# Routed experts with the weights as stationary operand: gate and up over 256 moving rows, gate factor applied when the result is copied

## What is computed

```python
def step(acc, blk):
    tok, g, e = blk                                  # 128 rows of one expert, their gates
    xb = xpad[tok]                                   # gather, 128 x 1024
    hid = jax.nn.silu(xb @ w_gate[e]) * (xb @ w_up[e])   # 128 x 256
    yb = (hid @ w_down[e]) * g[:, None]              # 128 x 1024
    return acc.at[tok].add(yb.astype(acc.dtype)), None
```

## Time and profile before

| | |
|---|---|
| median of 3 runs | 2429.33 us (2426.62 to 2432.03) |
| the profiled execution | 2434.02 us, span 2432.3 us |
| PE busy | 2247.8 us, 92% of the span |
| mean granted TensorE clock | 0.958 of 2.4 GHz |
| routed experts, steady part | about 1170 us to 2330 us |
| in it: PE, DVE, ACT, POOL busy | 100%, 64%, 59%, 37% |

### The profile page before, as it was taken

The page is one execution under the profiler, slowest core; times in us unless marked ns, Lnnn a source line. Parts: engine busy times, 40 slices in busy tenths (PEclk is TensorE's granted clock), DMA queues, the critical chain, the costliest instruction groups (busy, mean ns, idle before and its releaser), DMA issues. The chain is left out here.

```text
span 2432.3 us, 34810 instructions
## 1 busy us (share of the span) xinstructions
PE 2247.8 (92%) x10992; PEld 1825.9 (75%) x10992; DVE 1418.9 (58%) x2627; ACT 1115.7 (46%) x1803; POOL 649.8 (27%) x550
## 2 busy tenths in 40 slices
PE   7999999999949999984999999999999999999940
PEld 5777777777737888873888888888888888888840
DVE  5343334434346877773666666666666666666638
ACT  4342323334233333321555565565556655655533
POOL 1000000000011322332333343333333433333326
PEclk9999999999979999996999999999999999999975
DMA  5001000001372322324899999998999999899946
GB/s 207 32 32 37 26 33 26 33 26 34 110 182 80 104 95 79 102 78 157 261 281 287 284 276 283 286 277 278 282 291 271 284 281 290 270 287 283 286 115 241
DMA packets 198657, 435.85 MB, mean 179 GB/s; under 512 B 39584, under 2 KB 44176, under 8 KB 197296
## 3 DMA queue, kind: packets, MB, share of 16 engines
q1 hardware_dynamic: 155024, 289.49, 35.7%
q0 software_dynamic: 43600, 145.95, 22.4%
HBM read 328.16 MB, written 109.39 MB: 180 GB/s over the span
## 5 line engine op out<-in xcount | busy, mean ns | idle before, releaser
L1573 PE MATMUL ex_psU<-ex_guh,ex_xh 128*128 128x512 f32 x1024 | 411.4, 402 | 4.2 <-DVE ex_xl L1558 4.2
L1575 PE MATMUL ex_psU<-ex_guh,ex_xl 128*128 128x512 f32 x1024 | 402.1, 393 | 0.0
L1574 PE MATMUL ex_psU<-ex_gul,ex_xh 128*128 128x512 f32 x1024 | 401.4, 392 | 0.0
L1546 DVE TENSOR_TENSOR ex_gul<-ex_raw,ex_guh 128x1024 fp32r<-128x1024 f32 x256 | 299.2, 1220 | 41.1 <-ACT ex_guh L1496 41.1
L1422 POOL DMA_INDIRECT acc_d<-ex_y,ex_use x128 | 207.3, 1619 | 399.4 <-ACT ex_y L1485 343.6
L1496 ACT ACTIVATE ex_guh<-ex_raw 128x1024 fp32r<-128x1024 f32 x256 | 253.5, 1060 | 31.6 <-DMA ex_raw<-w_experts 31.6
L1573 PEld LDWEIGHTS ex_psU<-ex_guh,ex_xh 128*128 128x128 f32 x1024 | 193.5, 189 | 41.3 <-DVE ex_xl L1558 4.8
L1575 PEld LDWEIGHTS ex_psU<-ex_guh,ex_xl 128*128 128x128 f32 x1024 | 193.3, 189 | 41.0
L1574 PEld LDWEIGHTS ex_psU<-ex_gul,ex_xh 128*128 128x128 f32 x1024 | 193.8, 189 | 37.1
L1444 POOL DMA_INDIRECT ex_xg<-h_d,ex_ent x128 | 198.0, 1547 | 68.1 <-issue 38.1
L1573 PE MATMUL ex_psY<-ex_dnh,ex_hdh 128*128 128x512 f32 x512 | 210.3, 411 | 1.7 <-DVE ex_hdl L1529 1.7
(11 more groups left out here) (298 smaller groups left out, 4354.5 us busy)
## 6 DMA issues: line engine op xcount, KB each, us to landing
ex_raw<-w_experts SPq DMA_DIRECT2D x192, 1024.0 KB, 11.7
acc_d<-de_acc SPq DMA_DIRECT2D x19, 512.0 KB, 3.0
mi_xr<-xT SPq DMA_DIRECT2D x17, 512.0 KB, 3.5
de_cr<-cat SPq DMA_DIRECT2D x17, 512.0 KB
de_xr<-x_rows SPq DMA_DIRECT2D x17, 512.0 KB, 4.4
h_d<-de_h POOLq DMA_DIRECT2D x17, 512.0 KB, 6.2
ln_t<-acc_d SPq DMA_DIRECT2D x8, 1024.0 KB, 6.7
y<-ln_z SPq DMA_DIRECT2D x8, 1024.0 KB, 4.9
```

What stands on the lines that cost most here:

```text
L1546: V.tensor_tensor(lo, src, hi.bitcast(F32), ALU.subtract).then_inc(s_split, 1)
L1573: nc.tensor.matmul(out, lh, rh, start=start, stop=False)
L1574: nc.tensor.matmul(out, lh, rl, start=False, stop=False)
L1575: return nc.tensor.matmul(out, ll, rh, start=False, stop=stop)
```

## The change

The loop is written anew per expert instead of per block.

- Gate and up: the weights (`ex_guh`, `ex_gul`, 128x128) are now the stationary operand, and the 256 rows of both blocks (`ex_xh`, `ex_xl`) move. 96 matmuls of 256 columns per expert stand for 48 of 512. The result `ex_psU` has hidden units on partitions, in two halves `f`.
- Hidden is thereby already laid out as `down` wants it: the transposes L1581 and the tile `ex_psH` are gone. ACT rounds hidden out of SBUF.
- The gate no longer enters in VectorE's multiply. It is the scale of ACT's copy of `ex_psY` to `ex_y`, which is now four pieces of 512 columns per expert.
- `ex_xh`/`ex_xl` exist once for both blocks, no longer one per block parity; `ex_psX` exists twice, `ex_psY` has two halves that are handed over singly.
- PE's order per expert e: gate and up of e-1 (second half), the transposes of both blocks of e, down of e-2 (both blocks), gate and up of e (first half).
- The queues of POOL and SP keep their order.

```diff
-        psX, psU = ps("psX", [P, D]), ps("psU", [P, 2, 2 * FF])
-        psH, psY = ps("psH", [P, FC * P]), ps("psY", [P, D])
+        psX, psU, psY = ps("psX", [P, 2, D]), ps("psU", [P, FC, 2, BLK]), ps("psY", [P, 2, D // 2])
...
             def add_expert(e, b):
 
                 hold(pool, s_use, e + 1, s_passed)
                 for t in range(2):
-                    add_rows(2 * e + t, 2 * b + t)
+                    hold(pool, s_y, 4 * e + 2 * t + 2, s_passed)
+                    nc.gpsimd.indirect_dma_start(
+                        out=io["acc_d"], out_offset=bass.IndirectOffsetOnAxis(ap=use[:, 2 * b + t, 0:1].bitcast(U32), axis=0),
+                        in_=y[:, 2 * b + t, :], in_offset=None, compute_op=ALU.add).then_inc(s_add, 16)
...
+            def output(e, b, units):
+                if exists(e):
+                    for u in units:
+                        k, half = 2 * b + u // 2, u % 2
+                        act.wait_ge(s_dn, 4 * e + u + 1)
+                        if u == 0:
+                            act.wait_ge(s_use, e + 1)
+                            after(act, s_add, 32 * (e - 1))
+                        A(y[:, k, half * 512:(half + 1) * 512], psY[:, half, :], ACT.Copy,
+                          scale=use[:, k, 1:2].bitcast(F32)).then_inc(s_y, 1)
+
+            def pair(p, j):
+                for b in range(2):
+                    e = 2 * p + b
+                    sigmoid(e - 1, 0)
+                    round_w(p, e, b, (0, 1))
+                    hidden(e - 1, 0, 1 - b)
+                    round_w(p, e, b, (2, 3))
+                    sigmoid(e - 1, 1)
+                    round_x(e, 0)
+                    hidden(e - 1, 1, 1 - b)
+                    round_x(e, 1)
+                    output(e - 2, b, range(4))
+                    round_w(p, e, b, (4, 5))
...
-            def hidden_T(m, k):
-                pe.wait_ge(s_hid, m + 1)
-                pe.wait_ge(s_hl, m)
-                for f in range(FC):
-                    last = nc.tensor.transpose(psH[:, f * P:(f + 1) * P], hid[:, k % 2, f * P:(f + 1) * P], ident[:])
-                last.then_inc(s_hT, 1)
...
+            def transpose_x(p, e, b):
+                for t in range(2):
+                    pe.wait_ge(s_row[2 * b + t], 16 * (p + 1))
+                    after(pe, s_xl, 2 * e + t - 1)
+                    for kc in range(KC):
+                        last = nc.tensor.transpose(psX[:, t, kc * P:(kc + 1) * P], xg[:, 2 * b + t, kc * P:(kc + 1) * P], ident[:])
+                    last.then_inc(s_xT, 1)
...
-                    last = three(psU[:, k % 2, :], xh[:, k % 2, kc, :], xl[:, k % 2, kc, :],
-                                 guh[:, b, kc, :], gul[:, b, kc, :], kc == 0, kc == KC - 1)
+                for half in range(2):
+                    c0 = half * FF + f * P
+                    for kc in range(KC):
+                        last = three(psU[:, f, half], guh[:, b, kc, c0:c0 + P], gul[:, b, kc, c0:c0 + P],
+                                     xh[:, kc].rearrange("p s t -> p (s t)"), xl[:, kc].rearrange("p s t -> p (s t)"),
+                                     kc == 0, kc == KC - 1)
...
+            def pair(p, j):
+                for b in range(2):
+                    e = 2 * p + b
+                    gate_up(e - 1, 1 - b, 1)
+                    transpose_x(p, e, b)
+                    down(e - 2, b)
+                    gate_up(e, b, 0)
```

More of the change, by code:

```diff
@@ L1354, in stage_experts, with piece @@
         s_gu, s_sig, s_hid = sem("gate_up"), sem("sig"), sem("hid")
[L1355 to L1363, removed]
+        s_hh, s_hl, s_dn = sem("hid_hi"), sem("hid_lo"), sem("down")
+        def piece(b, q):
+            kind, part = q // 2, q % 2
             src = raw[:, b, kind, part * 1024:(part + 1) * 1024]
@@ L1369, in piece, with pairs @@
             return src, dnh[:, b, part, :], dnl[:, b, part, :]
[L1371 to L1376, removed]
+        def pairs(eng, pair):
+            for p in range(2):
+                pair(p, None)
+            with eng.Fori(2, PAIRS) as p:
+                pair(p, None)
             more = eng.value_load(ov[0:1, 2 * OVMAX:2 * OVMAX + 1], min_val=0, max_val=OVP)
@@ L1441, in pair @@
                         k = 2 * b + t
-                        if not first:
+                        if not (early and p == 0):
                             hold(pool, s_xT, 4 * p + k - 3, s_passed)
@@ L1523, in _ @@
+            e = 2 * pairs(act, pair)
+            sigmoid(e - 1, 0)
+            hidden(e - 1, 0, 1)
+            sigmoid(e - 1, 1)
+            output(e - 2, 0, range(2))
+            hidden(e - 1, 1, 1)
+            output(e - 2, 0, range(2, 4))
+            output(e - 1, 1, range(4))
         @block.vector
@@ L1568, in _ @@
+            e = 2 * pairs(dve, pair)
+            for f in range(FC):
+                activate(e - 1, f)
+                hidden(e - 1, f, 1)
         @block.tensor
@@ L1601, in down @@
+            def down(e, b):
+                if not exists(e):
+                    return
+                pe.wait_ge(s_hl, 2 * e + 2)
+                pe.wait_ge(s_split, 6 * e + 6)
+                for u in range(4):
+                    t, half = u // 2, u % 2
+                    after(pe, s_y, 4 * e + u - 1)
                     for f in range(FC):
-                        last = three(psY[:, cols], hdh[:, f, :], hdl[:, f, :], dnh[:, b, f, cols], dnl[:, b, f, cols],
+                        last = three(psY[:, half, :], hdh[:, b, f, t * P:(t + 1) * P], hdl[:, b, f, t * P:(t + 1) * P],
+                                     dnh[:, b, f, half * 512:(half + 1) * 512], dnl[:, b, f, half * 512:(half + 1) * 512],
@@ L1627, in _, with pair @@
-            end = pairs(pe, pair)
-            n = 4 * end
-            hidden_T(n - 2, 2)
-            gate_up(n - 1, 3, 1, 12 * end - 2)
-            down(n - 2, 1, 12 * end)
-            hidden_T(n - 1, 3)
-            down(n - 1, 1, 12 * end)
+                    last.then_inc(s_dn, 1)
+            def pair(p, j):
+                for b in range(2):
+                    e = 2 * p + b
+                    gate_up(e - 1, 1 - b, 1)
+                    transpose_x(p, e, b)
+                    down(e - 2, b)
+                    gate_up(e, b, 0)
@@ L1637, in stage_norm @@
+            e = 2 * pairs(pe, pair)
+            gate_up(e - 1, 1, 1)
+            down(e - 2, 0)
+            down(e - 1, 1)
 def stage_norm(nc, io):
```

209 lines of the change are left out of this document (75 added, 134 removed).

## The result

The changed kernel takes 2460.43 us (median; 2459.43 to 2463.49), the kernel before 2430.14 us beside it: ratio 1.0128, 95% interval [1.0111, 1.0146]. It is slower by 30 us, where 110 were forecast.

The account below looks back on a forecast made before the run. PE bounds the kernel before; a once-per-expert ring through adds and gathers was to replace it. (20.45 - 18.62) x 61 = 112 us, ends nothing on balance, gave 2540 us, range 2440 to 2680 us.

Parts of the forecast that it names:

- item 5: From the first gather's start to the second's landing, once per expert: taken as 10.0 us, from candidates 8.7, 9.8 and 12.3.
- the ring: Once per expert: transposes, down(e-2), copy, second add, two gathers, landing, next transposes; 20.05 us, 20.45 with the clock, bounding PE.
- PE's own work: PE's work per expert goes from 18.62 to 18.43 us, or 18.67; over 64 experts -12 to +3 us.
- items 1 to 3: Last down matmul's start to its copy's start 0.52 us, copy of 512 columns 0.6, copy's end to the add 0.84.
- item 4: On POOL, from the second add to the first gather: 1.91 us.
- item 7: On PE, 24 down matmuls up to the start of the last: 5.3 us.
- rival A: Gathers land early enough and PE stays the bound: 2417 us, or up to 2432; chance 0.14.
- The clock term: Waits before the second block's transposes halve the clock in one expert in four: 0.4 us per expert, bounds 0 and 1.6.
- The ends: Start +1.5 us for both blocks' transposes and split; at the end down's 1.7 us wait goes: nothing on balance.
- B: Gathers stay as slow as in the steady rows, adds and gathers sharing one queue: 2660 to 2760 us; chance 0.14.
- C: The weight load does not hide behind 256-column matmuls: 425 us more, 2855 us; chance 0.04.

Follow-up runs that it names:

- experiment 4: The kernel before with the down matmuls 256 columns wide instead of 512, twice as many: 2456.95 us, ratio 1.0094.
- experiment 10: The changed kernel with the indirect adds left out, POOL still waiting for y: 2437.38 us, ratio 1.0014 to the kernel before.
- experiment 1: The changed kernel with SP issuing an expert's weights ahead of its entries: 2660.93 us, ratio 1.0934 to the kernel before.
- experiment 9: The changed kernel with weights issued only when the gathers of the expert before have landed: 2490.32 us, ratio 1.0235 to the kernel before.
- 2: The changed kernel with POOL issuing the adds of e-3, not e-2, behind the gathers of e: 2556.72 us, ratio 1.0501 to the kernel before.
- 5: The changed kernel with the gathers of e+1 put ahead of the adds of e-2: 2565.01 us, ratio 1.049 to the kernel before.
- 6: The changed kernel with every engine reading the count of further blocks ahead of its loop: 2476.37 us, ratio 1.0117 to the kernel before.
- 8: The changed kernel with gathers of e+1 ahead of the adds of e-2 and weights ahead of the entries: 2620.31 us, ratio 1.0717 to the kernel before.
- 11: The changed kernel without the code for further blocks behind any engine's loop: 2457.37 us, ratio 1.0104 to the kernel before.
- 3: The kernel before with only the gate moved into the scale of ACT's copy of ex_psY: 2432.54 us, ratio 0.9999.
- 7: The kernel before with the input transposes moved directly ahead of the hidden transposes: 2445.66 us, ratio 0.9991.

## Why the prediction was wrong

The step that failed is item 5 of the ring, the gathers' landing: it took 10.0 us where 8.4 were measured, and so set the ring at 20.05 us, above PE's work, where it comes out at 18.5 us, below it. The ring that was forecast to take the bound from PE in every expert, +112 us, exceeds PE's work in 27 of 61 experts and costs 12.6 us. The ring itself is real, but the direction came out right in good part by luck: without the ring the kernel would still be slower, by PE's own work and the wait behind the loop, which the prediction had at -12 us and at nothing. Step by step:

- **PE's own work.** Between the two values it named (18.43 with 0.1175 us a matmul, 18.67 with 0.120), the second holds: 0.120 us in experiments 4, 10 and the changed kernel. Measured 18.737 us; the rest is that 16 transposes take 1.66 us, not 1.58. The choice of two was wrong, and so was the remark that the earlier trace rows would allow 0.120: with starts printed to 0.01 us they allow 0.116 to 0.119, and the router's matmuls do start every 0.118 us. The mistake was to carry their pace over to the experts' matmuls. It made PE's own part -12 us instead of +7.
- **The ring** is real. Its items 1 to 3 sum to 1.96 us as forecast (last down matmul 1711.99, second add 1713.95; the copy is 0.69 us, not 0.6, and it starts 0.43 us behind that matmul, not 0.52); item 4 is 1.88 us, item 7 is 5.32 us.
- **Item 5, the step that failed.** The first gather's start to the second's landing was taken as 10.0 us. It is 1.80 + 6.7 = 8.5 us with the median of all gathers, and 8.4 us on the median when taken pair by pair, since the second gather of a pair lands a little sooner. The text had seen that the weights move behind the gathers, and then took the price from the earlier trace rows, as if those rows were gathers without company. They were not: SyncE's row of before, shown below this list, has an expert's weights going out just ahead of and beside the first two of them. Without adds, gathers land in 5.2 us even with weights around them. The threshold named for rival A was 8.4 us, from PE's work of 18.43; with the measured 18.74 it is 8.7 us, and the measured 8.4 lies under it. So on the median rival A's mechanism holds.
- **The clock term** of 0.4 us per expert is zero in the changed kernel: short waits in some experts left the clock at 1.00. The mechanism isn't refuted: with the long waits of experiment 1 it costs 0.8 us per expert.
- **The ends**, "nothing on balance", were +9.6 us (+13.9 and -4.3). Of the 13.9, 6.8 are the wait behind the loop and the clock after it, 5.5 are the down matmuls that moved there and that the start, where PE waits, doesn't give back, and 1.6 are open. Nothing in the trace of before showed such a wait.

```profile
1127.64 11.45 SPq L1413 DMA_DIRECT2D ex_raw<-w_experts  x3
```

The ring's length follows the gathers' landing, with 1.96 + 1.88 + 1.80 + 0.9 + 5.3 = 11.8 us for all else:

| kernel | landing, median | ring by the sum | measured per expert |
|---|---|---|---|
| no adds (10) | 5.2 | none | 18.74 |
| changed | 6.7 | 18.5, under PE's 18.74 | 18.94 |
| weights behind gathers (9) | 7.6 | 19.4 | 19.32 |
| weights first (1) | 9.5 | 21.3 | 22.17 |

In experiment 9, where the ring is above PE's work and the clock stays at 1.00, the sum is good to 0.1 us. In experiment 1 it is 0.9 us short, and the lower clock in the ring's own PE work makes up 0.8 of that. In the changed kernel the median is 0.2 us under it, the spread of the landing (5.5 to 8.5 us) crosses it, and the mean excess of 0.2 us comes from the late ones alone. A forecast with single values can't give that: it says either nothing or the whole difference.

In all: PE's own work 7, gathers that land late 13, the ends 10, less 4 of the stages ahead, is the 25 us between the two traces. Between the medians it is 30 us; the 4 us of the stages ahead and some 3 of the 4.3 at the start belong to the two profiled executions and not to the change (that of before, 2434.0 us, is among that kernel's longer ones). Of rival A the bound was right in the middle of the distribution, and the late gathers and the ends were missing. B's price of 2660 us is what experiment 1 pays, but not for B's reason: in the changed kernel the two adds do come 2.7 us apart, and the gathers behind them land in 6.7 us. C is excluded: the loads hide at 0.120 us a matmul. Open are what in the jump costs the 4 us, and why experiment 10 has 2.3 us there. That wait is put down to DVE, but PE goes on 2.5 us after the start of an instruction transfer there too.

## What to carry to other kernels

Compute a new ring's length against the bound it would replace, and when they come within a microsecond, look at the spread of its slowest link, since late instances cost even where the median costs nothing. Take a transfer's landing time from rows with the same neighbours in flight as it will have after the change, and ask which transfers the change itself moves away. An order that frees one queue has to be followed once around: what releases the buffer that its first transfer reads?

## What the runs showed of the hardware

- The same gather of a block landed in 5.2 us (median) with no adds, 6.7 with adds ahead of it, 7.6 with earlier weights still running, 9.5 with weights issued beside it and 10.3 in the earlier trace rows. Indirect adds: 6.1 alone, 7.3 in the changed kernel, 11.2 to 11.7 behind gathers and weights.
- A 256-column matmul with a weight load of its own starts every 0.120 us in the experts (every 0.118 in the router's groups of eight), one of 512 columns every 0.228. The load hides in both. In the experts each matmul costs some 12 ns besides its columns, in down (experiment 4) as in gate and up.
- PE stood for 2.4 to 5.2 us behind the loop in kernels with 256-column matmuls and skipped code there (the changed kernel and experiments 1, 2, 4, 5, 6, 8 and 9), and not at all without the skipped code (11) or with 512-column matmuls only (before, 3, 7). In experiment 10 it is 2.3 us. That longer matmuls in PE's queue cover it is argued, not shown; in the kernel before, instruction transfers of 16 KB start at 2328.1 and 2332.2 us, and PE doesn't stop there.
- Short waits of PE (4.3 us in all in the changed kernel's steady part) left the granted clock at 1.00. With 104 us of waits between 1300 and 2300 us (experiment 1) it is 0.96 on the mean, with 105.8 us at 0.50, and those cost about 0.8 us in each expert.
